# Small experts in a mixture-of-experts decoder block: the up rows turned by eight 128x128 transposes, and their halves added on VectorE

## The reference, cut to what matters

```python
def moe_swiglu(h, w_router, b_router, w1, w3, w2):
    xt = h.reshape(N, D)
    logits = (xt @ w_router + b_router).astype(jnp.float32)
    top_val, top_idx = lax.top_k(logits, TOP_K)
    gates = jax.nn.softmax(top_val, axis=-1).astype(h.dtype)
    ...
    def run_block(args):
        tok, e = args
        xb = x_pad[tok]
        hb = jax.nn.silu(xb @ w1[e]) * (xb @ w3[e])
        return hb @ w2[e]
    ...
    out = jnp.zeros((N + 1, D), h.dtype).at[buf_tok].add(yb)[:N]
```

## Time and profile before

| What | Value |
|---|---|
| median of 3 runs | 1453.62 us |
| the profiled execution's own time | 1452.22 us |
| its span, first to last instruction | 1450.4 us |
| granted TensorE clock, mean | 0.997 |
| PE, DVE, ACT busy | 98%, 88%, 70% of the span |
| HBM read | 498.74 MB, 349 GB/s over the span |
| expert stage, roughly | 568 to 1436 us |

### The profile page before, as it was taken

One profiled execution on the slowest core, in us unless ns is written; L12 is line 12 of the kernel. 1 busy time (PEld: TensorE's weight loads), 2 busy tenths in 40 slices (PEclk: granted clock), 3 DMA queues, 4 the chain that ended last, 5 costly groups with the idle time before them and its releaser, 6 DMA issues.

```text
span 1450.4 us, 19280 instructions
## 1 busy us (share of the span) xinstructions
PE 1425.9 (98%) x7352; PEld 1205.8 (83%) x7352; DVE 1278.3 (88%) x1263; ACT 1019.1 (70%) x992; POOL 81.2 (6%) x109
## 2 busy tenths in 40 slices
PE   9999999999999999999999999999999999999996
PEld 5799889878889988888788878888888788888884
DVE  6899888977777768998999999999998999999995
ACT  3764454444567358778888888878879888888874
POOL 5000000000000000010000000100000010000010
PEclk9999999999999999999999999999999999999998
DMA  9849849987553757999999999999999999999993
GB/s 375 321 179 353 322 173 387 389 339 281 181 200 133 289 203 264 392 407 369 391 422 421 420 415 406 410 421 420 421 421 408 417 412 421 420 408 420 419 395 133
DMA packets 74277, 506.91 MB, mean 349 GB/s; under 512 B 8385, under 2 KB 8513, under 8 KB 16706
## 3 DMA queue, kind: packets, MB, share of 16 engines
q1 hardware_dynamic: 69986, 490.91, 84.3%
q0 software_dynamic: 4192, 14.70, 3.4%
HBM read 498.74 MB, written 6.83 MB: 349 GB/s over the span
## 4 chain that ended last, share of the span: by engine, by line
PE 67%; issue 19%; DVE 7%; DMA 3%; ACT 2%; POOL 1%; SPq 0%; DVEq 0%; ACTq 0%; POOLq 0%
PE ps L1993 17%; PE ps L1995 17%; PE ps L1994 17%; DVE lo L1292 4%; PE ps L2482 3%; PE ps L2481 3%; PE ps L2054 2%; DMA r<-in_moe_w_dram 2%; PE ps L2518 1%; ACT hi L744 1%; DMA gate_m<-rows_x,gather_row 1%; PE ps L2218 1%; PE ps L2201 1%; PE ps L2521 1%; DVE lo L1264 1%
## 5 line engine op out<-in xcount | busy, mean ns | idle before, releaser
L1292 DVE TENSOR_TENSOR lo<-raw,hi 128x2048 fp32r<-128x2048 f32 x245 | 552.8, 2286 | 27.2 <-ACT hi L744 26.2
L744 ACT ACTIVATE hi<-raw 128x2048 fp32r<-128x2048 f32 x245 | 464.9, 1917 | 41.1 <-DMA raw<-in_moe_w_dram 31.9
L1993 PE MATMUL ps<-hi,hT_hi 128*128 128x512 f32 (+3 forms) x896 | 349.6, 390 | 3.7 <-DVE hT_lo L1318 1.9
L1995 PE MATMUL ps<-hi,hT_lo 128*128 128x512 f32 (+3 forms) x896 | 343.0, 383 | 0.0
L1994 PE MATMUL ps<-lo,hT_hi 128*128 128x512 f32 (+3 forms) x896 | 342.3, 382 | 0.0
L1292 DVE TENSOR_TENSOR lo<-r,hi 128x2048 fp32r<-128x2048 f32 x91 | 206.6, 2286 | 10.7 <-ACT hi L744 10.7
L1264 DVE TENSOR_TENSOR lo<-raw,hi 128x2048 fp32r<-128x2048 f32 (+3 forms) x83 | 177.0, 2145 | 38.2 <-ACT hi L728 29.3
L1993 PEld LDWEIGHTS ps<-hi,hT_hi 128*128 128x128 f32 x896 | 168.4, 188 | 37.1 <-issue 4.5
L1995 PEld LDWEIGHTS ps<-hi,hT_lo 128*128 128x128 f32 x896 | 168.2, 188 | 32.3
L1994 PEld LDWEIGHTS ps<-lo,hT_hi 128*128 128x128 f32 x896 | 168.6, 188 | 29.5
L744 ACT ACTIVATE hi<-r 128x2048 fp32r<-128x2048 f32 x91 | 172.7, 1919 | 10.3 <-DMA r<-in_moe_w_dram 8.1
(11 more groups left out here) (352 smaller groups left out, 1786.2 us busy)
## 6 DMA issues: line engine op xcount, KB each, us to landing
raw<-in_moe_w_dram SPq DMA_DIRECT2D x245, 1024.0 KB, 11.2
r<-in_moe_w_dram SPq DMA_DIRECT2D x91, 1024.0 KB, 11.5
raw<-in_w_ada_dram SPq DMA_DIRECT2D x40, 1024.0 KB, 6.9
raw<-in_w_fd_dram SPq DMA_DIRECT2D x11, 1024.0 KB, 7.5
raw<-in_w_ga_dram SPq DMA_DIRECT2D x8, 1024.0 KB, 5.8
raw<-in_w_gb_dram SPq DMA_DIRECT2D x8, 1024.0 KB, 4.9
raw<-in_w_ab_dram SPq DMA_DIRECT2D x8, 1024.0 KB, 4.8
raw<-in_w_o_dram SPq DMA_DIRECT2D x8, 1024.0 KB, 5.8
```

Of the source, the lines that this page charges most:

```text
L744: act.activation(high_of(s), raw_of(r), ACT.Copy).then_inc(hi_done, 1)
L1292: dve.tensor_tensor(low_of(s), raw_of(r), high_of(s).bitcast(f32), ALU.subtract).then_inc(raw_done, 1)
L1993: pe.matmul(o, wh, mh, start=first, stop=False)
L1995: return pe.matmul(o, wl, mh, start=False, stop=last)
```

## The change

Small units alone are concerned. The turn becomes eight real transposes of 128x128: four of the gate rows into bank 2, then four of the up rows into bank 1 (which the up rows' copy has emptied). Each turned tile has the high-part sums in its first 64 columns and the low-part sums in the last 64. ACT copies the low halves of gate and of up into SBUF (`low_halves`), and DVE adds the high halves from PSUM (`gate_halves`, `up_halves`). The Silu then reads the gate sum and the product the up sum, both in SBUF. PE waits for the up addition before it writes w3 of the next unit into bank 1. `stack` and the POOL addition that made it are gone.

```diff
             def small_silu(n):
-                act.wait_ge(m_t, n + 1)
-                act.activation(h_small, ps[:, 2, 0:256].rearrange("p (c s) -> p c s", c=4), ACT.Silu).then_inc(m_st, 1)
+                act.wait_ge(m_ga, N_SMALL[n + 1])
+                act.activation(h_small, gate_sum, ACT.Silu).then_inc(m_st, 1)
...
+            def low_halves(n):
+                for bank, src, low, turned in ((2, m_gs, gate_sum, m_gl), (1, m_t, up_sum, m_ul)):
+                    act.wait_ge(src, N_SMALL[n + 1] if bank == 2 else n + 1)
+                    act.activation(low, ps[:, bank, :].rearrange("p (c s) -> p c s", c=4)[:, :, HALF_CAP:P], ACT.Copy).then_inc(turned, 1)
...
                 if n:
+                    if SMALL[n - 1]:
+                        low_halves(n - 1)
                     moe_hi(b + 2)
...
             def small_hidden(n):
                 dve.wait_ge(m_st, N_SMALL[n + 1])
-                dve.tensor_tensor(h_small, h_small, ps[:, 2, 256:512].rearrange("p (c s) -> p c s", c=4), ALU.mult).then_inc(m_sm, 1)
+                dve.wait_ge(m_ua, N_SMALL[n + 1])
+                dve.tensor_tensor(h_small, h_small, up_sum, ALU.mult).then_inc(m_sm, 1)
+
+            def gate_halves(n):
+                both = ps[:, 2, :].rearrange("p (c s) -> p c s", c=4)
+                dve.wait_ge(m_gl, N_SMALL[n + 1])
+                dve.tensor_tensor(gate_sum, gate_sum, both[:, :, 0:HALF_CAP], ALU.add).then_inc(m_ga, 1)
+
+            def up_halves(n):
+                both = ps[:, 1, :].rearrange("p (c s) -> p c s", c=4)
+                dve.wait_ge(m_ul, N_SMALL[n + 1])
+                dve.tensor_tensor(up_sum, up_sum, both[:, :, 0:HALF_CAP], ALU.add).then_inc(m_ua, 1)
...
                 if n:
                     moe_lo(b + 2)
-                    if not SMALL[n - 1]:
+                    if SMALL[n - 1]:
+                        gate_halves(n - 1)
+                        up_halves(n - 1)
+                    else:
                         hidden_lo(n - 1)
                 moe_lo(b + 3)
...
                 if SMALL[n]:
-                    pe.wait_ge(small_ready, 3)
-                    for z, src in enumerate((gate_s, up_s)):
+                    for bank, src in ((2, gate_s), (1, up_s)):
                         for c in range(4):
-                            at = z * 256 + c * HALF_CAP
-                            m = pe.matmul(ps[:, 2, at:at + HALF_CAP], src[:, c * P:(c + 1) * P], stack, start=True, stop=True)
+                            m = pe.transpose(ps[:, bank, c * P:(c + 1) * P], src[:, c * P:(c + 1) * P], ident[:, :])
+                        if bank == 2:
+                            m.then_inc(m_gs, 1)
...
+                if n and SMALL[n - 1]:
+                    pe.wait_ge(m_ua, N_SMALL[n])
                 unit_up(n, "w3")
```

More of the change, by code:

```diff
@@ L372, in build @@
         h_small = r2[:, 1024:1280].rearrange("p (c s) -> p c s", c=4)
-        stack = r2[:, 1280:1280 + HALF_CAP]
+        gate_sum = r2[:, 1472:1728].rearrange("p (c s) -> p c s", c=4)
+        up_sum = r2[:, 1728:1984].rearrange("p (c s) -> p c s", c=4)
         slots_s = r2[:, 1344:1344 + P]
@@ L472, in build @@
         m_up, m_st, m_sm = sem("m_up"), sem("m_st"), sem("m_sm")
+        m_gs, m_ga, m_ua = sem("m_gs"), sem("m_ga"), sem("m_ua")
+        m_gl, m_ul = sem("m_gl"), sem("m_ul")
         small_ready, experts_ready = sem("small_ready"), sem("experts_ready")
@@ L684, in _ @@
             pool.tensor_copy(slots_s[:, HALF_CAP:P], slots[:, 0:HALF_CAP]).then_inc(small_ready, 1)
-            pool.tensor_tensor(stack, ident[:, 0:HALF_CAP], ident[:, HALF_CAP:P], ALU.add).then_inc(small_ready, 1)
             pool.wait_ge(xn_out, 16)
@@ L1760, in select @@
                 if i >= LARGE:
-                    dve.wait_ge(small_ready, 3)
+                    dve.wait_ge(small_ready, 2)
                 for t in range(T):
```

## The result

The changed kernel takes 1479.39 us (median of 4 runs, 1479.12 to 1481.03) against 1453.8: a ratio of 1.0179, 95% interval 1.0162 to 1.0197. That is 25.6 us slower, where 19 had been forecast. The profiled execution took 1479.12 us.

What follows compares the result with a forecast made beforehand. PE, DMA and DVE were taken to stand within 4% of each other in the expert stage. A late lo adds 1.3 us to each of 15 pairs, +19 us on 1453.62, forecast 1473, range 1457 to 1485.

Steps and rivals of the forecast that it cites:

- The mechanism: After small turns: ACT's copies wait for PE, delaying hi, DVE's lo, then PE; +1.3 us per pair, +19; chance 0.75.
- lo of b+2: DVE's subtraction for chunk b+2 starts at T + 3.4, T being the first pass of a small unit's turn.
- Nine lo with the additions: DVE from lo of b+2 to the end of b+10: 21.76 us with four other instructions, plus 0.66 for additions.
- the tail: End of a pair: after lo of b+10, PE's 24 down matmuls of the large unit; next small turn 5.71 us later.
- The sum: Length of a late pair: 3.4 + 21.76 + 0.66 + 5.71 = 31.5 us, 31.8 to 31.9 with preparations, against 30.5.
- the case in the earlier trace: First small turn before the change: routing tables held DVE, lo of b+2 started at T + 3.52; that pair summed to 31.0 us.
- The spacing of transposes: PE's small turn: transposes 0.11 us apart though 0.27 long, eight costing 0.88; taken in turn, 2.2 and a 32.7 us pair.
- The DMA share: Sign of being right: in pairs the share falls under 1 and the rate to about 400 GB/s.
- the preparation of later experts: DVE work in the pairs: 14.2 us over 45 units, 0.6 us a pair, about half of it inside the chain.
- PE's saving: Small turns: 0.9 us less PE each, foretold to vanish; rival that it arrives: 19 us less, 1435, chance 0.04.
- Rival 2: Expert loads: DMA decides and raw buffers absorb ACT's wait, so the time is 1447 to 1454; chance 0.12.
- Triples: Small turns three units apart: DVE catches up in the extra large unit, 47.0 us as before within 1 us.

Runs made afterwards that it cites:

- The edit that should have confirmed this: Changed kernel with ACT's scaling of a later expert's gathered rows behind hi of b+6 instead of ahead of it: 1479.49 us against 1479.39.
- the mended one: Changed kernel with ACT's two copies of the low halves moved between hi of b+2 and hi of b+3: 1451.68 us, 0.999.
- the run that was to relieve DVE: Kernel with copies between the two hi, with ACT copying both halves and POOL adding instead of DVE: 1463.46 us, 1.0071.

## Why the prediction was right, and where its size was off

**The mechanism held at each step.** The transposes are 0.11 us apart and eight cost 0.88. The copies start at T + 0.63 (0.64 foretold) and hi of b+2 at T + 1.35 (1.43 foretold). lo of b+2 starts at T + 3.29 (3.4). Nine lo with the additions take 22.44 (22.42), the tail 5.70 (5.71), and a pair without preparations takes 31.4 (31.5). That was shown, not only argued: take the place of the copies away and the loss goes, put such a wait into the old kernel and the loss comes, shorten the wait by 0.43 us and 7 us come back, halve the loads and all but 0.9 us of the loss stays. The sum could be that close because the trace of before held the case in the earlier trace rows, a lo that was late for another reason.

**The spacing of transposes** was rightly taken from the trace. Four transposes lie between the starts of the two copies, which are 0.43 us apart, and eight passes delay the next matmul by 0.79 us. The granted clock stays at 1.00 in the windows with eight transposes. The Trainium skill (TensorE: Matmul & The Clock Gate, Part 4: PE-mode transpose) gives some 275 ns for a transpose; as a duration that agrees with the 270 to 273 ns here, as a distance between starts it does not.

**What did not come as foretold.** The DMA share stayed at 1.00 to 1.01 in the pairs, where it was to fall under 1, and the rate of about 400 GB/s showed in only one of two. Five pairs are longer than 32.2 us (up to 34.0) and two triples longer than 47.5.

**The term that was mis-sized** is the preparation of later experts, 0.3 us per pair in the sum. The 15 pairs measured 32.2 us in the mean, not 31.85, which is 5 us in all; one triple (780.2 to 829.7 us) took 49.5 instead of 47.3, and the five together 2.7 us more than before; of that triple's excess half loads take away 1.0, and what the rest is was not followed up. Among the pairs the excess sits in those with preparations. One such pair, between two turns on PE's timeline of the changed kernel:

```profile
1007.12 1.03 PE L2540 MATMUL ps<-ident,r 128*128 128x128 f32 x8
...
1040.46 1.03 PE L2540 MATMUL ps<-ident,r 128*128 128x128 f32 x8
```

Its 33.3 us have these parts: 31.4, plus 0.6 for DVE's own residue of gathered rows, plus 1.23 in which DVE waits for a hi that stands behind ACT's scaling. I had put only DVE's preparations into the chain. ACT's count as well, and the kernel before already showed it: in the same four pairs DVE waits there for the hi behind the scaling, 1.02 to 1.29 us each. This one stands in the pair from 993.92 to 1024.47 us:

```profile
1005.80 2.29 DVE L1292 TENSOR_TENSOR lo<-raw,hi 128x2048 fp32r<-128x2048 f32 x1 [1.29 <-ACT hi L744]
```

Since lo of b+2 started at T + 0.81 in it, the pair could still end in 30.5 us. In the changed kernel lo of b+2 starts at T + 3.29, and the wait comes on top. Seven of the 15 pairs have such a second wait of DVE for a hi, 5.8 us in all: four behind the scaling, three of 0.4 behind another instruction of ACT (L1071, 1.1 us long). The pairs missed 5. The edit that should have confirmed this left most of the wait in place; where it shortened the wait, the pair became shorter by as much. So the term rests on the traces of these two kernels, and no run without ACT's preparations confirms it.

**The rivals.** PE's saving did not arrive in the changed kernel at all, and at most 1.5 us of it in the mended one. The loads are one reason (a freed PE gains 4.8 us on half traffic). DVE and ACT in the pairs with preparations are the other by the traces; the run that was to relieve DVE could not show it, because POOL was slower. Rival 2, buffers that absorb the wait, is refuted by the half loads. Triples stayed within 1 us of before but for one. They were not free of the wait, though: with the copies behind one or both hi they average 46.5 and 46.3 us, against 47.6 in the changed kernel, so the wait takes from them what PE had saved.

## What to carry to other kernels

In a stream that is executed in order, ask of every moved instruction what stands behind it while it waits; the price is that of the first instruction behind it that another engine needs, not its own. Look in the trace of before for a place where that instruction was late for any other reason: it gives the price ready measured. Where three resources stand within some per cent of each other, as here, work taken off one of them is worth little (19 us of PE gave at most 1.5), and a new wait ahead of the shared chain costs what exceeds the slack: lo of b+2 came 2.5 us later in the pairs without preparations, and these became 1.8 us longer.

## What was not expected of the hardware

- DMA share: 1.01 at 405 GB/s over 300 us as well as at 421 in one pair. The share did not fall when the rate did; it fell to 0.65 only at 213 GB/s.
- A POOL addition of 128x256 in SBUF took 0.73 to 2.98 us, 2.4 in the median, where the 128x64 form had taken 0.33 and DVE takes 0.41. No run here shows why.
